# The first expert's tokens come from rows kept on chip, by one-hot products, and the rest of the routing tables is worked out behind them

## The reference, cut to what matters

```
def moe(h, w_router, b_router, w_gate, w_up, w_down):
    scores = sigmoid(t @ w_router)                        # 384 x 16
    best = argmax over 4 groups of the sum of its 2 best scores
    idx = the 2 best experts of that group
    w = scores[idx] / sum(scores[idx])
    ...
    hg = jnp.einsum('nd,edf->nef', t, w_gate)             # 1024 -> 512
    hu = jnp.einsum('nd,edf->nef', t, w_up)
    a = jax.nn.silu(hg) * hu * gate[..., None]
    y = jnp.einsum('nef,efd->nd', a, w_down)              # 512 -> 1024
```

## Time and profile before

| | us |
|---|---|
| median of 3 runs | 1155.25 |
| lowest and highest | 1152.99, 1155.74 |
| the profiled execution | 1150.34 |
| its span, first to last instruction | 1148.3 |
| TensorE busy | 1071.0 (93%) |
| VectorE busy | 851.7 (74%) |
| ScalarE busy | 689.6 (60%) |
| mean granted TensorE clock | 0.983 |

### The profile page before, as it was taken

How to read it: one execution, slowest core, us unless ns; L and a number is a source line. 1 busy time by engine, 2 the same in 40 slices (tenths; PEclk the granted TensorE clock), 3 DMA queues, 4 the chain that set the end, 5 groups by cost and what they waited for, 6 DMA issues and landing times.

```text
span 1148.3 us, 16078 instructions
## 1 busy us (share of the span) xinstructions
PE 1071.0 (93%) x5979; PEld 841.8 (73%) x5981; DVE 851.7 (74%) x1191; ACT 689.6 (60%) x866; POOL 153.0 (13%) x184
## 2 busy tenths in 40 slices
PE   6999988997999999999989998798799999999997
PEld 3798455673788888888869975477378888888886
DVE  5344656667789888888965556766779988889896
ACT  2424555543577778777734365654357777777764
POOL 0325100420011111111040011000001111111002
PEclk8999999998999999999999999999899999999998
DMA  9997899158689999999598381005768999999951
GB/s 351 341 348 235 327 275 302 38 217 323 221 311 367 368 378 372 373 375 382 225 374 262 119 264 47 1 1 208 300 228 334 371 382 372 372 375 371 373 200 57
DMA packets 82560, 319.86 MB, mean 279 GB/s; under 512 B 22464, under 2 KB 26926, under 8 KB 69692
## 3 DMA queue, kind: packets, MB, share of 16 engines
q1 hardware_dynamic: 67232, 285.58, 67.9%
q0 software_dynamic: 14160, 30.19, 7.7%
q10 hardware_dynamic: 1100, 3.23, 0.7%
HBM read 308.05 MB, written 30.57 MB: 295 GB/s over the span
## 4 chain that ended last, share of the span: by engine, by line
PE 77%; issue 7%; DVE 6%; ACT 4%; DMA 4%; SPq 1%; POOL 0%; ACTq 0%; DVEq 0%; POOLq 0%
PE bank L1209 16%; PE bank L1201 15%; PE bank L1202 15%; PE bank L919 3%; PE bank L915 3%; PE bank L912 3%; PE bank L1257 3%; PE bank L1092 2%; PE bank L1106 2%; ACT work L1599 2%; PE bank L984 2%; DMA ring<-in_w_in 2%; PE bank L889 2%; PE bank L1124 2%; PE bank L1025 1%
## 5 line engine op out<-in xcount | busy, mean ns | idle before, releaser
L1659 ACT ACTIVATE work_r<-ring 128x4096 fp32r<-128x4096 f32 x94 | 341.7, 3635 | 128.1 <-PE bank L1202 100.1
L2234 DVE TENSOR_TENSOR ring_r<-ring,work_r 128x4096 fp32r<-128x4096 f32 x92 | 404.0, 4417 | 0.0
L1201 PE MATMUL bank<-work_r 128*128 128x512 f32 x768 | 305.9, 398 | 3.0 <-issue 2.9
L1202 PE MATMUL bank<-work_r 128*128 128x512 f32 x768 | 300.3, 391 | 0.0
L1209 PE MATMUL bank<-ring_r,work_r 128*128 128x512 f32 x768 | 195.1, 396 | 5.0 <-DVE ring_r L2234 4.2
L1209 PEld LDWEIGHTS bank<-ring_r,work_r 128*128 128x128 f32 x768 | 143.9, 188 | 38.5 <-DVE ring_r L2234 5.0
L1201 PEld LDWEIGHTS bank<-work_r 128*128 128x128 f32 x768 | 145.2, 189 | 33.4 <-issue 3.1
L1202 PEld LDWEIGHTS bank<-work_r 128*128 128x128 f32 x768 | 144.7, 188 | 28.9
L2496 POOL DMA_INDIRECT work<-hscr,idx x32 | 35.8, 1119 | 379.5 <-PE bank L1257 261.2
L1515 ACT ACTIVATE work_r<-ring 128x512 fp32r<-128x512 f32 (+1 forms) x48 | 28.8, 603 | 70.5 <-PE bank L919 70.4
L1933 DVE TENSOR_TENSOR ring_r<-ring,work_r 128x512 fp32r<-128x512 f32 (+1 forms) x48 | 32.1, 677 | 49.2 <-ACT work_r L1515 49.2
(11 more groups left out here) (268 smaller groups left out, 1551.8 us busy)
## 6 DMA issues: line engine op xcount, KB each, us to landing
ring<-in_w_gate SPq DMA_DIRECT2D x32, 2048.0 KB, 10.3
ring<-in_w_up SPq DMA_DIRECT2D x32, 2048.0 KB, 10.8
ring<-in_w_down SPq DMA_DIRECT2D x32, 2048.0 KB, 10.6
ring<-in_w_ada SPq DMA_DIRECT2D x24, 2048.0 KB, 11.0
ring<-in_w_in SPq DMA_DIRECT2D x4, 2048.0 KB, 15.3
yscr<-hT POOLq DMA_DIRECT2D x2, 3072.0 KB, 13.1
ring<-yscr SPq DMA_DIRECT2D x6, 1024.0 KB, 7.3
ring<-in_w_out SPq DMA_DIRECT2D x4, 1280.0 KB, 6.8
```

Source lines behind the costliest of these rows:

```text
L1201: mm(b[:], x_hi[:, k, :], hi[:, k, half, :], start=(k == 0), stop=False)
L1202: last = mm(b[:], x_lo[:, k, :], hi[:, k, half, :], start=False, stop=False)
L1659: A_(w_hi[:, slot % 2, :], ring[slot][:], ACT.Copy).then_inc(s_hi, 1)
L2234: tt(ring_r[slot][:], ring[slot][:], w_hi[:, slot % 2, :].bitcast(F32), ALU.subtract).then_inc(s_lo, 1)
```

## The change

Expert 0 no longer waits for the indices and for the gather. DVE first writes an fp32 one-hot of expert 0's places (`onehot_first`: for each 128 tokens one comparison of 1 to 128 with the token's rank). TensorE multiplies the rows in `hrow` by it: for each of the 8 blocks of 128 features one sum over three blocks of tokens, 24 fp32 matmuls of 128 x 128 by 128 x 128. The result is expert 0's turned tokens, in the two banks where `tokens(0)` put them. For that all three `hrow` must stay, so two of them lie in `ysb`. POOL gathers from expert 1 on. `by_slot(0)` stands in the middle of the new matmuls, the adaLN jobs of `route[3]` stand behind them (on TensorE, ACT and DVE), 4 fillers are left of 30, and the tables of the other groups move back by one place each: groups 1 and 2 from the gate product to the up product of expert 0, group 3 and the gate weights to the gate product of expert 1. DVE's order follows.

```
@@ job_order
-        n += r[2] + ["rank"] + r[3]
-        order += [(l, j) for j in n]
+        n += r[2] + ["rank"]
+        order += [(l, j) for j in n] + [FROM_THIRD] + [(l, j) for j in r[3]]
@@ buffers
-        hrow = [grow[:, 0, :], grow[:, 1, :], carve(D, 2 * D)]
-        rlog = carve(T)
+        hrow = [grow[:, 0, :], ysb[:, 0, :], ysb[:, 1, :]]
+        rlog = carve(T, 3 * D)
+        onehot_first = c3(carve(T, 3 * D + 512), NT)
@@ TensorE
-                def jobs_done():
-
-                    for j in route[3]:
-                        ada(j)
-                    for bk in range(NB):
+                def jobs_done(taken):
+
+                    for bk in taken:
                         pe.wait_ge(s_evac[bk], sum(JOB[j][0] == bk for j in LIST[:LIST.index((l, "u0"))]))
...
-                    by_slot(0)
-                    if p == 0:
-                        jobs_done()
-
-                        for _ in range(24):
-                            mm(bG[:], onesb[:], swab[:], start=True, stop=True)
+                    def first_tokens():
+
+                        jobs_done((0, 1))
+                        pe.wait_ge(s_onef, l + 1)
+                        for t in range(NT):
+                            read_out(pe, (l, f"hr{t}1"))
+                        for k in range(KT):
+                            if k == KT // 2:
+                                by_slot(0)
+                            for t in range(NT):
+                                last = mm(bX[k // 4][:, (k % 4) * P:(k % 4 + 1) * P], hrow[t][:, k::KT], onehot_first[:, t, :],
+                                          start=(t == 0), stop=(t == NT - 1))
+                        last.then_inc(s_xt, 1)
...
-                    tokens(0, 0, g0 + 16)
-
-                    if p == 0:
-                        for _ in range(6):
+                    if p:
+                        by_slot(0)
+                        tokens(0, 0, g0 + 16)
+                    else:
+                        first_tokens()
+                        for j in route[3]:
+                            ada(j)
+                        jobs_done(range(2, NB))
+                        for _ in range(4):
                             mm(bU[:], onesb[:], swab[:], start=True, stop=True)
...
-                    gate_up(0, (0, 1), lambda: tokens(1, 1, g1 + 16), slots_in_gate, slots_in_up)
+                    gate_up(0, (0, 1), lambda: tokens(1, 1, g1 + 16), None, slots_in_up)
...
+                        if isinstance(i, int) and e == 1:
+                            gate_up(e, [place(u, kind)[0] for kind in range(2)], lambda: turn_a(0), slots_in_gate)
@@ ScalarE
-                for j in route[2] + route[3]:
+                for j in route[2]:
                     ada_row(l, j)
...
+                    if p == 0 and route[3]:
+                        tokens_upper(0)
+                        for j in route[3]:
+                            ada_row(l, j)
+                        upper(0, 1, 1)
+                    else:
+                        upper(0, 1, 1)
+                        tokens_upper(0)
@@ VectorE
+                    if p == 0:
+                        for t in range(NT):
+                            ins = ts(onehot_first[:, t, :], cv("iota"), rank[:, t * NE:t * NE + 1], None, ALU.is_equal)
+                        ins.then_inc(s_onef, 1)
+                        for j in route[2] if l else []:
+                            ada(l, j)
                     onehots(0)
-                    slots(0)
...
@@ GpSimd
                     for e in range(-2, NE + 2):
+                        if (p, e) == (0, -2):
+                            continue
```

More of the change, by code:

```diff
@@ L636, in gathers @@
         def gathers(l, p):
-            return (s_g, [l * k for k in G_PASS]) if p == 0 else (s_gf[l, p], [0, 0])
+            return (s_g, [l * G_FIRST[0] - 16, l * G_FIRST[1]]) if p == 0 else (s_gf[l, p], [0, 0])
         def scatters(l, p):
@@ L2269, in turned_rest @@
                         tt(aT_lo, bA[:].rearrange("p (k s) -> p k s", k=4), aT_hi.bitcast(F32), ALU.subtract).then_inc(s_as, 1)
-                    onehots(0)
-                    slots(0)
-                    if p == 0:
-                        for j in route[2] if l else route[3]:
-                            ada(l, j)
-                    if p:
-                        rest(0, 0, 0)
-                    for q in (1, 2):
-                        onehots(q)
+                    if p == 0:
[4 more added lines that the diff above has]
+                            ada(l, j)
+                    onehots(0)
                     if p == 0:
                         first_expert_low(1).then_inc(s_lo, 1)
+                    else:
+                        rest(0, 0, 0)
+                    slots(0)
                     if p == 0:
@@ L2286, in experts @@
                     tokens_rest(0)
+                    onehots(1)
+                    if p == 0:
+                        for j in route[3]:
+                            ada(l, j)
                     rest(0, 1, 1)
+                    onehots(2)
+                    tokens_rest(1)
                     onehots(3)
```

13 lines of the change are left out of this document (6 added, 7 removed).

## The result

The changed kernel takes 1161.75 us (median of five, 1159.96 to 1164.12), the one before 1155.25 in the same measurement (five, 1152.99 to 1156.85): a ratio of 1.0068, with a 95% interval of 1.0051 to 1.0085. It is 0.7% slower, where 0.6% faster was forecast.

The account below looks back on a forecast made before the run. TensorE was taken to bound the kernel (77% of the chain), idle before the first products. Gains of 2.9 and 6.4 less 2.0 made 7.3 us: 1155.25 to 1148.0 on the median, range 1144.5 to 1151.8.

Parts of the forecast that it names:

- The price of a product: New fp32 products for expert 0: 0.26 us each by L867, bounds 0.22 and 0.31; 24 take 6.2 at full clock.
- The prediction's own sign of being wrong: Among signs that would refute the forecast: the new products for expert 0 take 0.3 us or more each.
- The tokens were ready: Expert 0's turned tokens ready at 281.2 in layer 0 and 827.15 in layer 1; first products at 286.7 and 828.6.
- The moved tables: Low part of expert 1's gate chunk: DVE 1.0 us late in each layer, so 2.0 given back.
- starting the loop earlier should shift everything behind it: Expert loop: runs at TensorE's pace, loads move with it, so time won before the loop is kept.
- the 2.0 less 0.7 of the sum: 2.0 us given back by DVE's lateness; 0.7 won as layer 1's first product avoids half clock.
- the clock stays low longer: Rival, chance 0.15: during the new products full clock returns no earlier than 279.3 and 825.4; gain 3.9, time 1151.3.
- The gather of expert 1: POOL's first gather: issued at 278.9 and 826.45 as before, landing in time, no wait.
- the rivals' mechanisms: Clock low longer 0.15; clock never back 0.05 (1164); gather waits 0.05; DVE not late or no fall 0.15; loads bound 0.05.
- from tokens to first product: Between expert 0's tokens and the first product: 5.5 us in layer 0, 1.42 in layer 1.
- the wait of 2.08: Before the next low part, behind expert 1's: hangs on the turn of expert 0's output and stays 2.08 us.
- the 9.3 that the prediction gives without its lateness: Gain of 9.3 us if DVE is not late for expert 1's low part; within a rival of chance 0.15.

Follow-up runs that it names:

- experiment 1: The changed kernel with the new products reading 128 neighbouring elements of each row instead of every eighth: 1153.01 us, ratio 1.0002 to the kernel before.
- kernel 7: The changed kernel with rows kept in turned order, 8 tiny matmuls, and tables and weights back in expert 0's gate and up products: 1147.87 us, ratio 0.9938.
- experiment 12: Turned rows, early tables and 8 tiny matmuls, with ScalarE's copies stepping on the bank read and writing runs of 64: 1146.69 us, ratio 0.9932.

## Why the prediction was wrong

**The price of a product.** This is the step that failed: "A plain fp32 matmul of 128x128 by 128x128 is in the trace as L867", so 0.26, with bounds of 0.22 and 0.31. The price was right for L867's form and wrong for this read: 0.50, outside both bounds. The prediction's own sign of being wrong, 0.3 or more a product, came true. The tokens were ready 13.0 and 13.3 behind rank, where 8.9 and 9.6 were forecast, so first products came 4.1 and 3.7 late. Without the step they come at 14.92 and 10.13 (experiment 1). In the full kernel it is worth 8.2 us of rank to steady (117.7 against 109.5) and 0.8% of the time (1.0021 against 0.9938, both with early tables and 8 extra matmuls); with the tables as the change has them it is 0.5% (1.0068 against 1.0021, and 1.0029 against 0.9979). The trace of before holds one load with the same step, that of the turned tokens, but at 188 ns it looks like any other (L867's is 190); only with the rows turned (141 ns) does it show that it was slow too. First the kernel before, then kernel 7:

```profile
L1257 PEld LDWEIGHTS bank<-cst,work x256: 186/188/230, 287.1 to 1096.1; 128*128 128x128 f32 x128
L1268 PEld LDWEIGHTS bank<-cst,work x240: 138/141/226, 293.2 to 1093.2; 128*128 128x128 f32 x120
```

The Trainium skill (Advanced Engine Details and Errata, SBUF Cachelines, and SBUF — State Buffer, Door 1: The DMA port swizzle) has the rule that the prediction missed: lines of 16 bytes, full speed only if successive reads stay in a line, so fp32 with a step of up to 4. A step of 8 leaves the line at each element. The runs agree, with 336 against 193 ns; no run tried another step, so that the edge lies at 4 isn't shown here. The figure of the Trainium skill (TensorE: Matmul & The Clock Gate, Back-to-back issue gap) from which the prediction estimated 0.32 a product is above the 0.25 measured for contiguous rows and below the 0.50 of these.

**The moved tables.** The mechanism was right: a wait at the low part of expert 1's gate chunk, 0.67 and 0.69 against 1.0 forecast. Its size was wrong, since the prediction took a wait for its own length only. With the turned rows and 8 extra matmuls, early tables are worth 3.8 us of rank to steady (113.3 against 109.5). With the step of 8 they are worth 5.0 there (122.7 against 117.7), but the ratios (1.0029, 1.0021) don't separate. Each short wait can bring a stretch of half clock of 3.4, 1.7 us lost; the prediction knew that figure and kept it out of the sum. Not each one does: with 16 extra matmuls the changed kernel has the same wait of 0.69 in layer 1 and no fall behind it.

**What it didn't see.** It reads "starting the loop earlier should shift everything behind it", and that is right inside the loop. It had no term for TensorE code of another length, which moves a block's edge behind the branch: the second pause went from behind 20 matmuls to behind 4, the same shift that 16 extra matmuls give the kernel before. That cost 6.7 in the profiled execution. Over the placements, the change in its own form and without extra matmuls stands 0.4% above its two others, and its versions 0.4 to 0.5%; the kernel before, which in its own form is near its best, is from nothing to 1% slower in the other three.

**The miss by terms.** From the forecast 7.3 of gain to the 11.5 of loss between the profiled executions it is 18.8: 7.7 for the later first products (4.1 and 3.7), 4.4 between first product and steady (waits and falls of the clock beyond the 2.0 less 0.7 of the sum), 8.1 from steady to rank of layer 1, and -1.4 for the start and the end. Only the first two stretches are of what the prediction added up. With the right price for the products alone its sum would have been -0.4, no difference.

**The clock.** In layer 0 half clock lasted 6.8 (270.66 to 277.48), not the 3.4 forecast: of the rivals, "the clock stays low longer" came true there, but it cost nothing, since the slow loads set the pace at either level. In layer 1 the fall came only at 830.44, in the middle of the products. The gather of expert 1 was issued later behind rank than before (8.5 and 9.3 for 6.6 and 8.9), not "as before", and still nobody waited for it. The other terms held: 5.4 and 1.4 from tokens to first product (5.5 and 1.42), no wait for a gather in expert 0, the wait of 2.08 unchanged, the loop's period unchanged. "Slower" came with none of the rivals' mechanisms.

**What is then the change worth?** Averaged over 0, 8 and 16 extra matmuls the ratio is 1.0048 for the kernel before (1.0035 with its fourth placement, 24) and 1.0042 for the change. That is no difference, by three placements each that are up to 1% apart, so it isn't tight. Like with like it points both ways: where neither has a second pause the change is 0.3% slower (1.0028 and 1.0029 against 0.9997), and where both have it behind 4 matmuls it is 0.3% faster (1.0068 against 1.0102), and 0.3% is about the width of these intervals. In the stretch that it rebuilds it costs 2.3 to 4.8 us by the profiled executions with the same number of extra matmuls. Done with contiguous reads and early tables it gains 8.1, 10.0 and 9.5 there (0, 8 and 16 extra), near the 9.3 that the prediction gives without its lateness, and 12.3 with the copies of experiment 12 (8 extra). These versions stand at 0.9938, 0.9952 and 0.9932 with 8, 16 and 8 extra matmuls, but at 0.9991 with none: the gain of the repaired change and the loss at the branch are of one size.

Open: why the code lies as it does (which branch target meets which block's edge) wasn't derived from addresses, only from the shift; where the rest of the 1% of the kernel before with 16 extra matmuls comes from; and which short waits bring a fall of the clock and which don't stays unexplained, kernel by kernel.

## What to carry to other kernels

Before a matmul is priced from a row with the same shape, check the layout of its operand. The weights' side of an fp32 product with a step of 8 doubled its time, and laying the rows out once in the copy that writes them bought 0.5 to 0.8%; in that copy the step belongs on the read of the bank (1.08 for two copies), not on the write (1.93). When a change that alters the length of the code moves the time by less than 1%, time it with a few dummy instructions ahead too, and look at the "issue" rows behind each branch: here 16 idle matmuls moved the unchanged kernel by 1.0%. Small table work belongs where its engine waits anyway, because a wait of 0.7 us on TensorE is paid with 1.7 more when the clock falls behind it.

## What the runs showed of the hardware that was not expected

- A 128x128 fp32 weight load with a step of 8 elements takes 336 ns against 193 (medians), and the product 0.50 us against 0.25 at 2.4 GHz. With the step it is 0.50 at 1.2 GHz too.
- The branch past the further passes takes TensorE 6.0 to 7.0 us in layer 0, where the transfers are busy, of which 2.4 to 3.4 are idle time behind its queued matmuls; TensorE stands still a second time, until 5.7 to 6.0 behind the first instruction, when the second packet of code is wanted within the first 20 matmuls. In layer 1, with the transfers nearly idle, the branch takes 4.1 to 5.5 and the packets are 3.1 to 3.2 apart. The branches back inside the loop over experts take 0.26 at most and bring no packet of code.
- A fall of the granted clock lasted 3.4, 6.8 or 10.2 us, and once 13.7 at the start of an execution (8 extra matmuls in the kernel before); falls that run into the end of an execution are left out. The one of 581.27 to 591.51 followed the pauses behind the branch.
- ScalarE's copy of 128x512 fp32 from a bank takes 0.4 to 0.5 more when it writes with a step of 128 elements (1.93 to 2.06 for two against 1.06 to 1.09), and nothing more when it reads the bank with a step of 8 and writes in runs of 64 (1.08).
